# A hybrid DeltaNet and forgetting-attention block: fillings regrouped, and values turned by transposing instructions

## The reference

```
h = rmsnorm(x, norm_w);  proj = h @ w_in            # 1024 x 1024 by 1024 x 6168
qkv, z, b, a | q, k, v, z, f | gate_logit = split(proj)
y_a = gated_deltanet(...)      # 8 heads of 64, chunks of 64 tokens, scanned over 16 chunks
y_b = forgetting_attention(...) # 8 heads of 64, softmax(q k^T / 8 + c_t - c_s), causal
g_a, g_b = sigmoid(gate_logit + gate_b)
x = x + (g_a * (y_a @ w_up_gdn) + g_b * (y_b @ w_up_fox)) @ w_out
out = rmsnorm(x, final_norm_w)
```

## Time and profile before

| what | us |
|---|---|
| median of 3 runs | 968.0 (963.97 to 968.58) |
| the profiled execution | 967.72 |
| its span, first to last instruction | 965.9 |
| TensorE busy | 934.1 (97%) |
| VectorE busy | 611.2 (63%) |
| ScalarE busy | 446.5 (46%) |
| mean granted TensorE clock | 0.995 |

### The profile page before, as it was taken

How to read it: one execution, slowest core, us unless ns; L and a number is a source line. 1 busy time by engine, 2 the same in 40 slices (tenths; PEclk the granted TensorE clock), 3 DMA queues, 4 the chain that set the end, 5 groups by cost and what they waited for, 6 DMA issues and landing times.

```text
span 965.9 us, 16052 instructions
## 1 busy us (share of the span) xinstructions
PE 934.1 (97%) x6484; PEld 702.7 (73%) x6484; DVE 611.2 (63%) x981; ACT 446.5 (46%) x778; POOL 19.7 (2%) x28
## 2 busy tenths in 40 slices
PE   4999999999999999999989999999999999999997
PEld 3778787788888876766765665665666888888885
DVE  7387568799999824464476786785773434246252
ACT  7465654533433414532646636456354533334131
POOL 1000002020000000000000000000000000000000
PEclk9999999999999999999999999999999999999999
DMA  8111351249223482322453325225123331223162
GB/s 249 40 45 47 94 174 47 68 156 215 89 89 103 138 244 74 100 67 78 138 178 103 110 98 152 80 97 156 34 66 120 121 110 58 85 109 110 28 199 79
DMA packets 115745, 104.89 MB, mean 109 GB/s; under 512 B 34192, under 2 KB 95760, under 8 KB 115288
## 3 DMA queue, kind: packets, MB, share of 16 engines
q1 hardware_dynamic: 104008, 80.27, 29.8%
q10 hardware_dynamic: 10512, 19.40, 5.5%
q0 software_dynamic: 1152, 4.19, 1.3%
HBM read 76.84 MB, written 27.00 MB: 108 GB/s over the span
## 4 chain that ended last, share of the span: by engine, by line
PE 44%; DVE 4%; ACT 2%; issue 1%; DVEq 0%; ACTq 0%
PE pj L2117 6%; PE pj L2119 5%; PE pj L2118 5%; PE pc L2248 3%; PE pa L2216 3%; PE pa L2185 1%; PE pj L2128 1%; PE pj L2130 1%; PE pj L2129 1%; DVE qk L1849 1%; PE pb L2263 1%; DVE pa L1899 1%; PE pc L2384 1%; PE pc L2383 1%; PE pb L2384 1%
## 5 line engine op out<-in xcount | busy, mean ns | idle before, releaser
L144 PE MATMUL pj<-h_hi,w_hi 128*128 128x512 f32 x504 | 204.2, 405 | 1.4 <-ACT xc L641 0.9
L145 PE MATMUL pj<-h_lo,w_hi 128*128 128x512 f32 x504 | 197.4, 392 | 0.0
L146 PE MATMUL pj<-h_hi,w_lo 128*128 128x512 f32 x504 | 197.1, 391 | 0.0
L144 PEld LDWEIGHTS pj<-h_hi,w_hi 128*128 128x128 f32 x504 | 94.8, 188 | 25.0 <-issue 2.4
L146 PEld LDWEIGHTS pj<-h_hi,w_lo 128*128 128x128 f32 x504 | 94.9, 188 | 20.4
L145 PEld LDWEIGHTS pj<-h_lo,w_hi 128*128 128x128 f32 x504 | 95.0, 188 | 18.0 <-issue 0.2
L2117 PE MATMUL pj<-h_hi,w_hi 128*128 128x512 f32 x248 | 103.2, 416 | 0.3 <-PEq L315 0.3
L2119 PE MATMUL pj<-h_hi,w_lo 128*128 128x512 f32 x248 | 97.0, 391 | 0.0
L2118 PE MATMUL pj<-h_lo,w_hi 128*128 128x512 f32 x248 | 96.8, 390 | 0.0
L641 ACT ACTIVATE xc<-pj 128x512 f32<-128x512 f32 x40 | 24.0, 600 | 108.3 <-PE pj L146 107.8
L2117 PEld LDWEIGHTS pj<-h_hi,w_hi 128*128 128x128 f32 x248 | 46.5, 188 | 22.0 <-issue 12.9
(11 more groups left out here) (355 smaller groups left out, 1840.2 us busy)
## 6 DMA issues: line engine op xcount, KB each, us to landing
w_raw<-in_w_in SPq DMA_DIRECT2D x48, 512.0 KB, 4.4
fox_scratch<-xc ACTq DMA_DIRECT2D x40, 256.0 KB, 2.8
qkv<-in_x SPq DMA_DIRECT2D x8, 512.0 KB, 6.5
fa<-rows_scratch POOLq DMA_DIRECT2D x8, 512.0 KB, 5.0
rv<-fr_scratch SPq DMA_DIRECT2D x16, 256.0 KB, 4.0
ma<-m_scratch SPq DMA_DIRECT2D x8, 512.0 KB, 4.1
rv<-in_w_out SPq DMA_DIRECT2D x8, 512.0 KB, 3.7
w_raw<-in_x SPq DMA_DIRECT2D x8, 512.0 KB, 4.5
```

The costliest lines, as they stand in the source:

```text
L144: nc.tensor.matmul(o, w_hi[:, slot, k], h_hi[:, k, cols], start=(k == 0), stop=False)
L145: nc.tensor.matmul(o, w_hi[:, slot, k], h_lo[:, k, cols], start=False, stop=False)
L146: last = nc.tensor.matmul(o, w_lo[:, slot, k], h_hi[:, k, cols], start=False, stop=(k == KT - 1))
```

## The change

- The values are turned by transposing instructions: 16 of 64x64 for each pair of chunks, both halves of the rows to partitions 0-63, the second half's in bank 1 of `pc`. ScalarE's scaling becomes 16 copies of 64x64 in place of 8 of 128x64, the second half's going from partitions 0-63 to 64-127. `tok3` has a fourth plane, so that the factors of both halves lie on partitions 0-63.
- The first spill of tile 13 is staged in `state` in place of `fst`, and doesn't have the wait on the convolution. The zeroing of `state` moves two iterations later in VectorE's stream, behind a wait for that store.
- The low part of tile 28 moves from before VectorE's first `chunk` to after it.
- `FILLS`: the openings of pairs 0, 2 and 3 have ten fillings in place of eight (pair 1 keeps eight), in all pairs as a group of 3 ahead of score piece 2, and the rest (7, or 5 in pair 1) behind score piece 3. Taken away are one filling at v = 9 and one at v = 11 of pair 0, one at v = 11 of pairs 1 and 3, two at v = 11 of pair 2.
- `square_sums(p - 1, 1)` in step v = 1 moves behind that step's first filling and score piece 7.

```diff
--- before.py
+++ after.py
@@ -160,7 +160,7 @@
         mq = sb("mq", [P, 4, C], where=st)
         rr = sb("rr", [P, 3, C], where=st)
         tokq = sb("tokq", [P, 3, C], where=st)
-        tok3 = sb("tok3", [P, 3, 2 * NT, PAIRS], where=st)
+        tok3 = sb("tok3", [P, 4, 2 * NT, PAIRS], where=st)
         gl = sb("gl", [P, 2 * NT, PAIRS], where=st)
         glr = sb("glr", [P, 1, C], where=st)
         glv = sb("glv", [P, 1], where=st)
@@ -635,13 +635,16 @@
                 def take_spill(n, half):
 
                     act.wait_ge(pj_done, 2 * n + half + 1)
-                    if n == N_Z:
+                    stage = fst[:, half]
+                    if n == N_Z and half == 0:
+                        stage = state[:, 0:2].rearrange("p n a d -> p (n a d)")
+                    elif n == N_Z:
                         act.wait_ge(conv_step, CONV * N_CONV)
                     act.wait_ge(fox_stored[half], 16 * (n - N_Z))
-                    nc.scalar.activation(fst[:, half], pj[:, half], ACT.Copy).then_inc(pj_free, 1)
+                    nc.scalar.activation(stage, pj[:, half], ACT.Copy).then_inc(pj_free, 1)
                     act.wait_ge(pj_free, 2 * n + half + 3)
                     act.dma_start(fox_dram[spill_row(n):spill_row(n) + P, HALF * half:HALF * half + HALF],
-                                  fst[:, half]).then_inc(fox_stored[half], 16)
+                                  stage).then_inc(fox_stored[half], 16)
 
                 def tile_operands(t):
                     act.wait_ge(k_turned, t + 1)
@@ -653,8 +656,10 @@
                     act.wait_ge(v_turned1, t + 1)
                     for x in (2 * t, 2 * t + 1):
                         for p in range(PAIRS):
-                            last = nc.scalar.activation(vt[:, p, chunk_cols(x)], pc[:, 0, chunk_cols(PAIRS * (x % 2) + p)],
-                                                        ACT.Copy, scale=tok3[:, 2, x, p:p + 1])
+                            for b in range(2):
+                                last = nc.scalar.activation(vt[half_rows(b), p, chunk_cols(x)],
+                                                            pc[half_rows(0), b, chunk_cols(PAIRS * (x % 2) + p)],
+                                                            ACT.Copy, scale=tok3[half_rows(0), 2 + b, x, p:p + 1])
                     last.then_inc(kv_scaled, 1)
 
                 for n in range(N_Z, N_G):
@@ -851,7 +856,7 @@
                     if n == 12:
                         dve.wait_ge(tok_mm, 1)
                         nc.vector.tensor_copy(tok3[:, :, :, :].rearrange("p n x a -> p (n x a)"),
-                                              pc[:, 0, 0:3 * C])
+                                              pc[:, 0, 0:4 * C])
                         nc.vector.tensor_copy(gl[:, :, :].rearrange("p n a -> p (n a)"), pc[:, 1, 0:C])
                     if n == 11:
                         dve.wait_ge(mq_loaded, 64)
@@ -876,7 +881,6 @@
                     nc.vector.tensor_tensor(qt[:, :, tok_cols(t)], qt[:, :, tok_cols(t)], er_slot(t),
                                             ALU.mult).then_inc(qg_done, 1)
 
-                nc.vector.memset(state[:, 0], 0.0).then_inc(s_done, 1)
                 dve.wait_ge(kk_stored[0], 64)
                 dve.wait_ge(kk_stored[1], 64)
                 dve.wait_ge(ssq_mm, 2)
@@ -886,8 +890,11 @@
                 spread(de, 1, rr[:, 2], rr[:, 1], de_spread)
 
                 for n in range(N_Z, N_G):
-                    if n > N_Z:
+                    if N_Z < n < N_G - 1:
                         split_lo(dve, n + 2, n % 2)
+                    if n == N_Z + 2:
+                        dve.wait_ge(fox_stored[0], 16)
+                        nc.vector.memset(state[:, 0], 0.0).then_inc(s_done, 1)
                     if KQ_AT <= n < KQ_AT + NT:
                         tile_scores(n - KQ_AT)
                     substitute(SUB_AT.get(n, 0))
@@ -946,6 +953,8 @@
 
                 for t in range(NT):
                     chunk(t, 0)
+                    if t == 0:
+                        split_lo(dve, N_G + 1, (N_G + 1) % 2)
                     if 0 < t <= PAIRS:
                         z_plus(t - 1)
                     if t == 4:
@@ -1054,9 +1063,9 @@
                         pe.wait_ge(kk_out, 4)
                         perm = ident[:, :].rearrange("p (b a n) -> p b n a", b=2, a=PAIRS)
                         for b in range(2):
-                            for m in (0, 2):
-                                nc.tensor.matmul(pc[half_rows(b), 0, C * m:C * m + C], tokq[:, m], perm[:, b],
-                                                 start=True, stop=True)
+                            nc.tensor.matmul(pc[half_rows(b), 0, 0:C], tokq[:, 0], perm[:, b], start=True, stop=True)
+                            nc.tensor.matmul(pc[half_rows(0), 0, chunk_cols(2 + b)], tokq[:, 2], perm[:, b],
+                                             start=True, stop=True)
                             for p in range(0, PAIRS, 2):
                                 nc.tensor.matmul(pc[half_rows(side(b, p)), 0, C:2 * C].rearrange("p (n a) -> p n a", a=PAIRS)[:, :, p:p + 2],
                                                  tokq[:, 1], perm[:, b, :, p:p + 2], start=True, stop=True)
@@ -1091,9 +1100,8 @@
                         for x in (2 * t, 2 * t + 1):
                             for p in range(PAIRS):
                                 for b in range(2):
-                                    last = nc.tensor.matmul(pc[half_rows(b), 0, chunk_cols(PAIRS * (x % 2) + p)],
-                                                            vt[half_rows(b), p, chunk_cols(x)], ident[half_rows(b), half_rows(b)],
-                                                            start=True, stop=True)
+                                    last = nc.tensor.transpose(pc[half_rows(0), b, chunk_cols(PAIRS * (x % 2) + p)],
+                                                               vt[half_rows(b), p, chunk_cols(x)], ident[half_rows(b), half_rows(b)])
                         last.then_inc(v_turned1, 1)
 
                 done = [0]
@@ -1307,7 +1315,10 @@
         STEPS = PER * PAIRS
         TAIL = 4
         AHEAD = 32
-        FILLS = ((8,) + (4,) * 4 + (0, 4) * 4) * PAIRS + (5, 4, 4, 3)
+        FILLS = ((10,) + (4,) * 4 + (0, 4, 0, 4, 0, 3, 0, 3)
+                 + (8,) + (4,) * 4 + (0, 4, 0, 4, 0, 4, 0, 3)
+                 + (10,) + (4,) * 4 + (0, 4, 0, 4, 0, 4, 0, 2)
+                 + (10,) + (4,) * 4 + (0, 4, 0, 4, 0, 4, 0, 3) + (5, 4, 4, 3))
         UNIT = KT + PAIRS
         A_FILLS = KT * 2 * UNIT
         RAW0 = 16 * (N3 // 2 + 1) + 16 * (SMALL_DMAS - 1)
@@ -2312,12 +2323,11 @@
                         weight_sums(p - 1, 1)
                     max_scores(p, 0)
                     max_scores(p, 1)
-                    fill(2)
+                    fill(3)
                     max_scores(p, 2)
                     turn_values(p, 0)
-                    fill(1)
                     max_scores(p, 3)
-                    fill(5)
+                    fill(FILLS[PER * p] - 3)
                     turn_max(p, 0)
                     for v in range(4):
                         max_scores(p, 4 + 2 * v)
@@ -2327,10 +2337,10 @@
                             turn_values(p, 1)
                         else:
                             values(p, v - 1)
+                        fill(1)
+                        max_scores(p, 5 + 2 * v)
                         if v == 1 and p:
                             square_sums(p - 1, 1)
-                        fill(1)
-                        max_scores(p, 5 + 2 * v)
                         fill(3)
                     turn_max(p, 1)
                     for v in range(4, SLOTS, 2):
@@ -2348,7 +2358,7 @@
                             values(p, v - 1)
                         if v == 8:
                             square_sums(p, 0)
-                        fill(4)
+                        fill(FILLS[PER * p + v + 2])
                         if v == 4 and p + 1 < PAIRS:
                             head_sums(p + 1)
                 values(PAIRS - 1, SLOTS - 2)
```

## The result

The changed kernel takes 970.65 us (median of 12 runs, 969.5 to 974.86), the kernel before 967.91 in the same series: a ratio of 1.0037, 95% interval 1.0023 to 1.005. That is 2.7 us slower by the medians: under 0.5%, but with twelve runs each the whole interval lies above 1. (The ratio is not the quotient of the two medians, here 1.0028; the two measures can differ by about 1 us.

The account below looks back on a forecast made before the run. TensorE, busy 97% of the span, was taken to bound the kernel. Terms -3.6 - 1.8 + 0.1 - 3.4 + 8.85 = +0.15 us gave 967.8 from 967.7, no measurable change; own range 965 to 971, full range 961.5 to 973.

Parts of the forecast that it names:

- New waits: 3.2 + 3.7 + 0.85 + 0.7 + 0.2 + 0.2 = 8.85: TensorE waits from regrouped fillings: `gated` in pairs 0 and 3, a score piece, ends of pairs 0 and 3, stream changes.
- Transposing turn: Turning the values in eight tiles: row halves run side by side, taking what the keys' turn takes, 3.6 us saved.
- Rival 1: In the values' turn, the transposing pairs don't overlap, so 3.6 us are missing: 971.4 us; chance 0.15.
- rival 3: In the values' turn, 64-column transposing instructions neither pair nor are shorter than full ones: 976.7 us; chance 0.08.
- ScalarE's copies: Scaling the turned values: 8 copies more per tile at 0.225 us each, 1.8 us, fit ScalarE's idle time; cost 0.
- Chunk order: At the first `through`: moving tile 28's low part behind VectorE's first chunk removes a 1.79 us wait; gain 1.8 us.
- Openings: Pair openings: two more fillings cover the wait at the turn of the maxima in pairs 0, 2, 3; gain 3.4 us.
- Waits for gated: Step v = 0 of pairs 0 and 3: up fillings come before their `gated`; 3.2 and 3.7 us lost, restart included.
- Rival 2: The 3.2 and 3.7 us waits don't come, as `gated` is earlier or fillings are miscounted: 960.9 us; chance 0.17.
- Score piece 7 of pair 2: Step v = 1: without `square_sums` ahead, the piece waits about 1.0 us for `row_max` of piece 6; 0.85 us more.
- End of pair 0: After v = 11: one filling less means 0.7 us more waiting at the sums, which already wait 0.33 for VectorE.
- First half: Values' turn, ScalarE's copies, staging and chunk order together: a gain of 5.3 us.

Follow-up runs that it names:

- the spare matmuls: The changed kernel with 27 unneeded matmuls right ahead of its two long waits for `gated` (12 in pair 0, 15 in pair 3): 967.51 us against 968.07, ratio 1.0004.

## Why the prediction was wrong, point by point

**The step that failed** is the one that read "New waits: 3.2 + 3.7 + 0.85 + 0.7 + 0.2 + 0.2 = 8.85" and then added it as if a microsecond of waiting cost a microsecond. The waits are there and nearly of that size. What the sum lacks is the price of the half clock behind the two long ones, a term that it put at nothing without a reason: 3.2 us by the spare matmuls. With TensorE kept streaming through the waits the time is 967.51; without, 970.65. That 967.51 is so near to the forecast's 967.8 is partly luck, since the smaller errors listed below nearly cancel. So is that 970.65 lies inside the forecast's own range of 965 to 971, which was made up of late inverses, drains and half a microsecond on each wait, and had nothing of the clock. The stretch in the kernel before was open to be read and was not: the granted clock is 0.995 in the mean, and 1.6 us behind the 1.79 us wait of the earlier trace rows it is half for 3.4 us.

The Trainium skill (TensorE: Matmul & The Clock Gate, Part 1) says that the throttled state of the array's clock is the default and that activity releases it. The traces agree: each half-clock stretch between the first 60 us and the last matmul begins in or up to 1.6 us behind a wait of TensorE's of 1.8 us or longer.

Term by term, from the profile after:

- **Transposing turn, -3.6:** right in mechanism, too large: busy time falls from 8.8 to 5.1 us, but 0.11 us more at each change from the keys' turn to the values' leaves 2.8. The prediction named a price of this kind, for the change of tiling mode, and left it out of the sum. Whether the 0.11 is that, or the change to transposing instructions, no run tells apart. Rival 1 (no pairing) and rival 3 (dearer instructions) are refuted: a pair takes 56 ns.
- **ScalarE's copies, 0:** wrong in size. I took 0.225 us each from the earlier trace rows; they start 0.32 apart, 5.13 us for a tile and not 3.6. It cost one wait of 0.31 us, at the tile whose weights land late.
- **Staging, 0:** the wait at tile 14 is 0.94 as before, right.
- **Chunk order, -1.8:** right in mechanism, too small: the wait's stretch of half clock goes too (3.0 us in all for this edit). The inverses were in time. What I did not price is the next load in the queue, z: 1.14 us at the second tile's `through` in this profile, 0.28 in the one with spare matmuls. With z loaded first that wait is gone.
- **Openings, -3.4:** right; L2213 waits in pair 1 alone (1.34).
- **Waits for gated, 3.2 and 3.7 with the restart:** measured 2.94 and 3.50 of idle time, right. Rival 2, that they don't come, is refuted.
- **Score piece 7 of pair 2, +0.85:** 1.03 against 0.16, right, and it goes when `square_sums` goes back. **End of pair 0, +0.7:** 0.62 at the sums (0.33 before) and 0.17 at the values, so some 0.5.
- **First half, -5.3:** measured -5.5 (-4.5 by the ratio), the right size by terms that cancel: a smaller turn and the waits for z and ScalarE on one side, the stretch at 355 us on the other.
- **A slip in the range:** it is said to take in most of rival 2, whose 960.9 lies below its lower end of 961.5.

Up to the second block the change was ahead by 4.6 us (the first score piece at 483.2 in place of 487.8). At the output product it was behind by 6.0 (876.4 against 870.4). Between them lie +10.6 us where I had 5.4. In this profile the waits alone are 4.2 more than before, and the two stretches are up to 5.9. In executions in which the stretches are shorter they cost less; that this is most of the difference between this profile and the median fits the granted clocks (0.994 in executions of 969.74 and 970.43 us, 0.988 in that of 974.86) but isn't shown for single stretches.

Still open: why a stretch is 3.4 us in one execution and 6.8 in another at the same wait. The profiles show only that it was 6.8 us when it began before the wait ended (three cases, 0.7 to 1.2 us before) and 3.4 when it began after (nine cases).

## What to carry to other kernels

Filling a stall by moving work is only half the question: number the moved pieces and check, for each that itself waits, whether its provider still comes first. A long wait of TensorE must be priced with the clock that follows it, and the granted clock just behind the waits that exist is the place to read this from. If such a wait can't be avoided, matmuls that nobody needs can be cheaper than idleness: 27 of them gained 3.2 us here. And busy time doesn't show what lies between two groups of instructions: read the distance from the start of one group to the start of the next.

## What the runs showed of the hardware that I had not expected

- The clock fell at every one of the eight waits of 2.25 to 3.5 us in five profiles (three times before the wait ended, five times up to 1.2 us after), the start of the kernel left aside, behind four of seven waits of 1.8 us at the first `through`, and behind none of 1.4 us or less in the second block.
- ScalarE's short copies started 0.197 us apart while successive ones stayed on the same half and bank, 0.315 to 0.34 us apart at a change.
- Two transposing instructions on different row halves run side by side though both write partitions 0-63, each into its own bank: 128 in 5.1 us, starts 3 to 4 ns apart within a pair and 56 ns from pair to pair.
- The first transposing instruction after the identity matmuls of the keys' turn started 0.11 us later than an identity matmul did there (0.58 against 0.46 us from the start of the keys' turn).
